# A modulation GEMV moves from GpSimd to VectorE, and four products start on the K tiles that are ready

## The reference, cut to what matters

```python
c_act = jax.nn.silu(c)
mod = c_act @ w_mod[l] + b_mod[l]          # w_mod: 2 x 2048 x 6144
shift, scale, gate = jnp.split(mod, 3, axis=-1)
h = x * (1.0 + scale[:, None]) + shift[:, None]
# and once more for the shared keys and values:
mod = c_act @ w_mod_kv + b_mod_kv          # 2048 x 4096
```

## Time and profile before

| what | value |
|---|---|
| median of three runs | 2972.42 us |
| span of the profiled execution (first to last instruction) | 2965.1 us |
| TensorE matmul busy | 2702.1 us, 91% |
| VectorE busy | 1774.0 us, 60% |
| ScalarE busy | 1222.6 us, 41% |
| GpSimd busy | 1637.6 us, 55% |
| moved by DMA | 604.67 MB, mean 204 GB/s |

### The profile page before, as it was taken

How to read it: one execution, slowest core, us unless ns; L and a number is a source line. 1 busy time by engine, 2 the same in 40 slices (tenths; PEclk the granted TensorE clock), 3 DMA queues, 4 the chain that set the end, 5 groups by cost and what they waited for, 6 DMA issues and landing times.

```text
span 2965.1 us, 37109 instructions
## 1 busy us (share of the span) xinstructions
PE 2702.1 (91%) x12005; PEld 2128.3 (72%) x12005; DVE 1774.0 (60%) x1786; ACT 1222.6 (41%) x1575; POOL 1637.6 (55%) x1060
## 2 busy tenths in 40 slices
PE   7987999998899888888888999998999879999987
PEld 6765787876677666666666777766788768888876
DVE  5789867757455555455545666655457556545645
ACT  4354333335333433333333333333458444444643
POOL 6986777774038999999989877798200000000000
PEclk9999999999999999999999999999999989999999
DMA  7776676776466777777676767766654536565453
GB/s 228 221 227 215 204 236 198 212 226 226 152 189 216 223 226 224 223 223 222 219 224 224 241 224 244 226 225 223 210 163 145 177 109 207 181 210 172 125 184 132
DMA packets 312714, 604.67 MB, mean 204 GB/s; under 512 B 26590, under 2 KB 28644, under 8 KB 310668
## 3 DMA queue, kind: packets, MB, share of 16 engines
q1 hardware_dynamic: 301628, 571.92, 61.5%
q10 hardware_dynamic: 10960, 31.10, 2.8%
HBM read 592.31 MB, written 10.62 MB: 203 GB/s over the span
## 4 chain that ended last, share of the span: by engine, by line
PE 42%; POOL 36%; issue 9%; DVE 8%; DMA 2%; ACT 2%; POOLq 1%; SPq 1%; DVEq 0%; ACTq 0%
POOL gemv_w L497 19%; POOL gemv_acc L507 14%; PE bank L566 12%; PE bank L568 11%; PE bank L567 11%; DVE w_lo L1649 3%; PE bank L654 2%; POOL gemv_acc L495 1%; PE bank L530 1%; POOL gemv_lo L511 1%; DVE sq L1795 1%; POOL gemv_hi L505 1%; DMA gemv_w<-in_kv_w_mod 1%; DMA raw<-in_w_ffn_down 1%; ACT w_hi L1067 1%
## 5 line engine op out<-in xcount | busy, mean ns | idle before, releaser
L1649 DVE TENSOR_TENSOR w_lo<-raw,w_hi 128x1024 fp32r<-128x1024 f32 x820 | 1252.2, 1532 | 1087.1 <-ACT w_hi L1067 1069.1
L1067 ACT CAST w_hi<-raw 128x1024 fp32r<-128x1024 f32 x820 | 860.1, 1050 | 1593.3 <-PE bank L568 815.1
L497 POOL TENSOR_TENSOR gemv_w<-gemv_w,small 128x512 f32<-128x512 f32 x480 | 735.9, 1533 | 183.8 <-DMA gemv_w<-in_w_mod 161.2
L507 POOL TENSOR_TENSOR gemv_acc<-gemv_acc,gemv_w 128x512 f32<-128x512 f32 x480 | 766.3, 1596 | 72.5 <-POOL gemv_w L497 68.9
L566 PE MATMUL bank<-w_hi,u_hi 128*128 128x512 f32 x1408 | 586.2, 416 | 93.2 <-DVE w_lo L1649 86.5
L568 PE MATMUL bank<-w_hi,u_lo 128*128 128x512 f32 x1408 | 564.2, 401 | 0.0
L567 PE MATMUL bank<-w_lo,u_hi 128*128 128x512 f32 x1408 | 563.7, 400 | 0.0
L566 PE MATMUL bank<-w_hi,s_hi 128*128 128x512 f32 x1280 | 520.8, 407 | 19.8 <-DVE w_lo L1649 16.6
L568 PE MATMUL bank<-w_hi,s_lo 128*128 128x512 f32 x1280 | 509.4, 398 | 0.0
L567 PE MATMUL bank<-w_lo,s_hi 128*128 128x512 f32 x1280 | 509.1, 398 | 0.0
L566 PEld LDWEIGHTS bank<-w_hi,u_hi 128*128 128x128 f32 x1408 | 269.4, 191 | 207.4 <-DVE w_lo L1649 138.7
(11 more groups left out here) (337 smaller groups left out, 2289.2 us busy)
## 6 DMA issues: line engine op xcount, KB each, us to landing
gemv_w<-in_w_mod SPq DMA_DIRECT2D x384, 256.0 KB, 3.0
raw<-in_w_in SPq DMA_DIRECT2D x176, 512.0 KB, 4.1
raw<-in_a_w_in SPq DMA_DIRECT2D x128, 512.0 KB, 3.9
raw<-in_w_ffn_gate SPq DMA_DIRECT2D x88, 512.0 KB, 4.3
raw<-in_w_ffn_up SPq DMA_DIRECT2D x88, 512.0 KB, 3.8
raw<-in_w_ffn_down SPq DMA_DIRECT2D x88, 512.0 KB, 4.2
gemv_w<-in_kv_w_mod SPq DMA_DIRECT2D x128, 256.0 KB, 3.0
raw<-in_kv_w SPq DMA_DIRECT2D x64, 512.0 KB, 3.7
```

The source lines that it names most:

```text
L497: pool.tensor_tensor(gemv_w[:, k % 2], gemv_w[:, k % 2], c_k, ALU.mult).then_inc(gemv_scaled, 1)
L507: ins = pool.tensor_tensor(gemv_acc[:], gemv_acc[:], gemv_w[:, k % 2], ALU.add)
L1067: act.copy(w_hi[:, s], raw[:, s]).then_inc(hi_done, 1)
L1649: dve.tensor_tensor(w_lo[:, s], raw[:, s], w_hi[:, s].bitcast(F32), ALU.subtract).then_inc(lo_done, 1)
```

## The change

The GEMV leaves GpSimd, which is then empty. VectorE does one step behind each split: one fused multiply and add from `gemv_w` into `gemv_acc` (a plain multiply for the first K tile; for the last one a second product for `gemv_hi`, and the subtraction for `gemv_lo`). SyncE's queue issues the GEMV load of step k behind the raw load two units later (`GEMV_LAG` = 2), and the last two of a chunk behind the first two raw loads of the next body or product. `load_gemv` itself, its wait included, is as before.

At the four borders `finish` is gone. The last chunk's drain stands at the end of the product like any other; its turn stands on TensorE behind unit 1, 2 or 3 of the next product, its cuts on ScalarE and VectorE before the splits of iteration 2 to 4, and TensorE waits for `turn_free` only before unit 6 (before unit 20 in down).

The core of the diff (the same is done on SyncE for every product, and for ffn, down and v2 on ScalarE and VectorE as it stands here for w_out):

```diff
@@ -325,7 +325,7 @@
...
-        gemv_scaled, gemv_cut = sem("gemv_scaled"), sem("gemv_cut")
+        gemv_cut = sem("gemv_cut")
...
+
+        GEMV_LAG = 2
...
@@ -432,87 +434,91 @@
                     sp.wait_ge(gemv_step, i * (pr.mods * KD) + (n * KD + k - 1))
                 sp.dma_start(gemv_w[:, k % 2], w[k * P:(k + 1) * P, ds(col + m * COLS, COLS)]).then_inc(gemv_landed[k % 2], 16)
...
-            def wide_body(pr, i, w, col, mod_w=None, mod_col=None):
+            def gemv_of(pr, i, mod_w, mod_col):
+
+                def issue(j):
+                    load_gemv(pr, i, j, mod_w, mod_col)
+
+                return issue
+
+            def tail_of(pr, gemv):
+
+                def issue(j):
+                    gemv(pr.units - GEMV_LAG + j)
+
+                return issue
+
+            def gemv_behind(j, gemv, tail):
+
+                if j >= GEMV_LAG:
+                    gemv(j - GEMV_LAG)
+                elif tail:
+                    tail(j)
+
+            def wide_body(pr, i, w, col, gemv, tail):
 
                 half = pr.units // 2
                 for j in range(pr.units):
                     load(pr, i, j, w, j % half, col + (j // half) * COLS)
-                    load_gemv(pr, i, j, mod_w, mod_col)
+                    gemv_behind(j, gemv, tail)
+
...
             pr = products["qkv"]
-            wide_body(pr, 0, w_in[0], 0, w_mod_2[0], 0)
+            gemv0 = gemv_of(pr, 0, w_mod_2[0], 0)
+            wide_body(pr, 0, w_in[0], 0, gemv0, None)
             with sp.Fori(1, pr.bodies) as i:
-                wide_body(pr, i, w_in[0], i * 2 * COLS, w_mod_2[0], i * COLS)
+                wide_body(pr, i, w_in[0], i * 2 * COLS, gemv_of(pr, i, w_mod_2[0], i * COLS),
+                          tail_of(pr, gemv_of(pr, i - 1, w_mod_2[0], (i - 1) * COLS)))
+            last = tail_of(pr, gemv_of(pr, pr.bodies - 1, w_mod_2[0], (pr.bodies - 1) * COLS))
             pr = products["spill"]
...
+            none = gemv_of(pr, 0, None, None)
+            two_weights(pr, 0, (w_branch_gdn, w_branch_moba), none, last)
+            with sp.Fori(1, pr.bodies) as i:
+                two_weights(pr, i, (w_branch_gdn, w_branch_moba), none, None)
...
-        @block.gpsimd
-        def _(pool):
-            pool.wait_ge(signal("c_ready"), 1)
-
-            def gemv_chunk(i):
-
-                for k in range(KD):
-                    pool.wait_ge(gemv_landed[k % 2], i * (8 * KD) + 16 * (k // 2 + 1))
-                    c_k = c_act[:, k:k + 1].broadcast_to([P, COLS])
-                    if k == 0:
-                        if not isinstance(i, int):
-                            pool.wait_ge(gemv_cut, i * 2)
-                        ins = pool.tensor_tensor(gemv_acc[:], gemv_w[:, 0], c_k, ALU.mult)
-                    else:
-                        pool.tensor_tensor(gemv_w[:, k % 2], gemv_w[:, k % 2], c_k, ALU.mult).then_inc(gemv_scaled, 1)
-                        pool.wait_ge(gemv_scaled, i * (KD - 1) + k)
-                        pool.wait_ge(gemv_step, i * KD + k)
-                        if k == KD - 1:
-
-                            if not isinstance(i, int):
-
-                                pool.wait_ge(mod_stored, i * 16)
-                            pool.tensor_tensor(gemv_hi[:], gemv_acc[:], gemv_w[:, k % 2], ALU.add).then_inc(gemv_cut, 1)
-                            pool.wait_ge(gemv_cut, i * 2 + 1)
-                        ins = pool.tensor_tensor(gemv_acc[:], gemv_acc[:], gemv_w[:, k % 2], ALU.add)
-                    ins.then_inc(gemv_step, 1)
-
-                pool.wait_ge(gemv_step, i * KD + KD)
-                pool.tensor_tensor(gemv_lo[:], gemv_acc[:], gemv_hi[:].bitcast(F32), ALU.subtract).then_inc(gemv_cut, 1)
-
-            gemv_chunk(0)
-            with pool.Fori(1, MOD_CHUNKS) as i:
-                gemv_chunk(i)
...
@@ -549,13 +555,15 @@
                     src.parity = (first + q) % 2
                     turn(i * pr.turns + (first + q), src)
 
-            def chunk(pr, i, x, hi, lo, units, between=None):
+            def chunk(pr, i, x, hi, lo, units, between=None, cut_by=None):
 
 
                 if not (isinstance(i, int) and pr.body0 + i == 0):
                     pe.wait_ge(drained[x], i * 2 + 2 * pr.body0)
                 for u in range(units):
                     j = x * units + u
+                    if cut_by and j == cut_by[0]:
+                        pe.wait_ge(turn_free, cut_by[1])
...
@@ -870,49 +874,58 @@
             branch_body(0)
             with pe.Fori(1, pr.bodies) as i:
                 branch_body(i)
-            turn_mixed(pr.bodies - 1)
-            pe.wait_ge(turn_free, pr.turn0 + pr.bodies * pr.turns)
+
+            def last_mixed(j, pr=pr):
+                if j == 1:
+                    turn_mixed(pr.bodies - 1)
+
+            mixed_cut = (6, pr.turn0 + pr.bodies * pr.turns)
...
+            def last_x(name, dest):
+
+                pr = products[name]
                 c = 2 * pr.bodies - 1
                 pe.wait_ge(drained[c % 2], 2 * (pr.body0 + c // 2 + 1))
                 turn_x(products[dest], c)
-                pe.wait_ge(turn_free, products[dest].turn0)
...
+                    if j == 2 and first:
+                        last_x("w_out", "ffn")
+                    elif j == 3 and not first:
                         turn_stage(pr, i - 1, 1)
 
-                chunk(pr, i, 0, u2_hi, u2_lo, pr.units // 2, due)
+                chunk(pr, i, 0, u2_hi, u2_lo, pr.units // 2, due, (6, pr.turn0) if first else None)
...
-            turn_stage(pr, pr.bodies - 1, 1)
-            pe.wait_ge(turn_free, pr.turn0 + pr.bodies * pr.turns)
...
-            turning_x("down", hid_hi, hid_lo, "v2", lambda: mod_columns(0))
+            def down_first(j, pr=pr):
+
+                if j == 3:
+                    turn_stage(pr, pr.bodies - 1, 1)
+                if j == products["down"].units // 2 - 1:
+                    mod_columns(0)
+
+            turning_x("down", hid_hi, hid_lo, "v2", down_first, (KF // 2 - 2, pr.turn0 + pr.bodies * pr.turns))
...
-            plain("v2", s_hi, s_lo)
+            plain_body("v2", 0, s_hi, s_lo, lambda j: j == 2 and last_x("down", "v2"), (6, products["v2"].turn0))
+            plain_body("v2", 1, s_hi, s_lo)
...
@@ -1648,6 +1677,36 @@
                 dve.wait_ge(hi_done, i * pr.units + (pr.unit0 + RING + j + 1))
                 dve.tensor_tensor(w_lo[:, s], raw[:, s], w_hi[:, s].bitcast(F32), ALU.subtract).then_inc(lo_done, 1)
 
+            def gemv(pr, i, j):
+
+                if not pr.mods:
+                    return
+                part = pr.units // pr.mods
+                m, k = j // part, j % part
+                if k >= KD:
+                    return
+                n = pr.mod0 + m
+                c_k, w_k = c_act[:, k:k + 1], gemv_w[:, k % 2]
+                dve.wait_ge(gemv_landed[k % 2], i * (pr.mods * 8 * KD) + (n * 8 * KD + 16 * (k // 2 + 1)))
+                if k == 0:
+                    if not (isinstance(i, int) and i * pr.mods + n == 0):
+                        dve.wait_ge(gemv_cut, i * (pr.mods * 2) + 2 * n)
+                    dve.tensor_scalar(gemv_acc[:], w_k, c_k, None, ALU.mult).then_inc(gemv_step, 1)
+                    return
+                dve.wait_ge(gemv_step, i * (pr.mods * KD) + (n * KD + k))
+                if k == KD - 1:
+                    if not (isinstance(i, int) and i * pr.mods + n == 0):
+
+                        dve.wait_ge(mod_stored, i * (pr.mods * 16) + 16 * n)
+                    dve.scalar_tensor_tensor(out=gemv_hi[:], in0=w_k, scalar=c_k, in1=gemv_acc[:], op0=ALU.mult,
+                                             op1=ALU.add).then_inc(gemv_cut, 1)
+                dve.scalar_tensor_tensor(out=gemv_acc[:], in0=w_k, scalar=c_k, in1=gemv_acc[:], op0=ALU.mult,
+                                         op1=ALU.add).then_inc(gemv_step, 1)
+                if k == KD - 1:
+                    dve.wait_ge(gemv_step, i * (pr.mods * KD) + (n * KD + KD))
+                    dve.wait_ge(gemv_cut, i * (pr.mods * 2) + (2 * n + 1))
+                    dve.tensor_tensor(gemv_lo[:], gemv_acc[:], gemv_hi[:].bitcast(F32), ALU.subtract).then_inc(gemv_cut, 1)
+
             def body(name, i, drain, between=None, limit=UNITS, finish=None):
 
 
@@ -1656,10 +1715,14 @@
                 for j in range(pr.units):
                     if between:
...
                     if between:
                         between(j)
-                    if finish and j == pr.units - 2:
+                    ending = finish and j == pr.units - 2
+                    if ending:
+                        gemv(pr, i, j)
                         finish()
                     if not isinstance(i, int) or pr.unit0 + i * pr.units + RING + j < limit:
                         split(pr, i, j)
+                    if not ending:
+                        gemv(pr, i, j)
                     if j % half == half - 1 and not (finish and j == pr.units - 1):
```

(58 more changed lines are left out.)

69 lines of the change are left out of this document (38 added, 31 removed).

## The result

The changed kernel takes 5024.61 us (median of four runs, 5021.69 to 5027.45) against 2972.04 us for the kernel before (median of four): ratio 1.690, 95% interval 1.688 to 1.692. The forecast was 5009 us, slower, in a range of 4750 to 5360.

The account below looks back on a forecast made before the run. SyncE's one in-order queue carries weights and GEMV loads, so TensorE, 91% busy, waits; after the change 500 rounds of 7.7 us (3850) + 22 + 1129 outside = 5001, plus 7.3 above the span: 5009 us, range 4750 to 5360.

Parts of the forecast that it names:

- The closed loop: SyncE's queue and VectorE's order: next raw load waits for the previous unit's landing, cast, split and GEMV step; chance 0.62.
- The round: One unit through that loop, from GEMV issue to step done: 7.7 us, bounds 7.3 to 8.4, where TensorE needs 2.93.
- The links: Raw loads each held by the split before, from qkv to q2: 500 at 7.7 us, 3850 us.
- free runs: Four stretches of 8 units in down without GEMV steps, outside the loop: 17 us each, 68 us.
- Rival (C): TensorE joins the loop in spill at the lower clock: 64 us more, 5073 us; chance 0.25.
- the rounding products: VectorE's one more product of 0.69 us ahead of the counted step in each of 32 chunks: 22 us.
- (A): Loop not closed, GEMV fits VectorE's idle time, weights flow at TensorE's pace: 2794 us, faster; chance 0.05.
- (B): Order wrong by one, two raw loads in flight per round: 3.85 us a unit, 3083 us; chance 0.04.
- (D): The extra wait is always met and the pace stays: 2972 us; chance 0.01.
- the queue's release: SyncE's queue no longer late, weights at TensorE's pace in qkv, w_out, ffn, down, v2 and k2: gain 148 us.
- The borders: Four idle stretches of 38 us between products; only 7.4 us credited, at the border from branch to w_out.
- What surrounds the span: Median of the runs taken as 7.3 us above the profile page's span: 5001 becomes 5009 us.

Follow-up runs that it names:

- lags four and six: Changed kernel with each GEMV load four or six units behind its raw load instead of two: 2777.61 us with four, 2775.87 us with six.
- lag three: Changed kernel with each GEMV load three units behind its raw load instead of two: 3185.69 us.
- the last experiment: Changed kernel with GEMV loads three units behind, but their wait for the step made ahead of the raw load of that position: 4670.46 us.

## Why the prediction was right, point by point

**The closed loop** was read off the program order and is there as described: one raw load per round, never two; undone by lags four and six, halved by lag three and (in the FFN) by another order on VectorE, kept by the last experiment.

**The round.** 7.7 us forecast, bounds 7.3 to 8.4. Measured between two raw loads in the first FFN body, 1795.28 - 1787.98 = 7.30; over the whole FFN 7.76 a unit. The fused step was priced 0.69 from another line, and 0.05 before it; it takes 0.745, of which 0.09 lies over the end of the split, so it adds 0.66 where 0.74 was forecast. In the first body, which is written out and not in a loop, the GEMV load goes 0.04 us after the step's end and the raw load 0.38 after it. Over the whole FFN these are 0.15 and 0.57 by the mean, against 0.15 and 0.60 forecast, and that is most of why this body is quicker than the rest. From the issue of a raw load to its cast are 4.07 us by the mean in the FFN and 4.25 in spill, where the forecast had 3.8 + 0.09: the term that was too small. By the median the landing took 3.8 to 4.2 (instruction, count, KB, median us to landing), beside the earlier trace rows:

```profile
gemv_w<-in_w_mod SPq DMA_DIRECT2D x384, 256.0 KB, 2.7
raw<-in_w_in SPq DMA_DIRECT2D x176, 512.0 KB, 4.2
...
raw<-in_w_ffn_gate SPq DMA_DIRECT2D x88, 512.0 KB, 4.0
raw<-in_w_ffn_up SPq DMA_DIRECT2D x88, 512.0 KB, 3.8
```

**The links.** The split of a unit is counted on L1678 (length of the stretch, busy time and count, which leaves out units 0 to 3):

```profile
0.00:1418.90 1418.90, 213.28 (x175) 0.76 0.36 113
0.00:1570.20 1570.20, 254.68 (x209) 0.78 0.37 116
0.00:3282.40 3282.40, 526.60 (x431) 0.76 0.35 109
0.00:3672.00 3672.00, 616.73 (x505) 0.76 0.35 112
0.00:4147.20 4147.20, 692.70 (x567) 0.76 0.35 111
```

| stretch, by splits | forecast | measured |
|---|---|---|
| unit 4 to 178, 174 links | 1347 | 1418.9 - 40.7 = 1378.2 |
| 178 to 212, branch | 149.8 | 1570.2 - 1418.9 = 151.3 |
| 212 to 434, 222 links | 1719 | 3282.4 - 1570.2 = 1712.2 |
| 434 to 508, 42 links and 4 free runs | 393 | 3672.0 - 3282.4 = 389.6 |
| 508 to 570, 62 links | 480 | 4147.2 - 3672.0 = 475.2 |
| from unit 570 | 870.8 | 5019.9 - 4147.2 = 872.7 |

(The forecast column is the text's 7.7 a link and 0.69 a chunk's end, with 11, 14, 3 and 4 chunk ends in the linked stretches.) All rows but the first are within 7 us. The first is 31 us over, and all of it is in spill: qkv's links, from the split of unit 4 to that of unit 48, took 340.4 us, and 340 follow from the forecast's terms. The other rows together are 12 us under, so the sum hits closer (0.3%) than its largest row does, and that part is luck.

**Rival (C)**, that TensorE joins the loop in spill at the lower clock, had 0.25 and 64 us. The clock fell as it said, to 0.76 in spill. But TensorE did not join. In the FFN five casts waited for it, 29.9 us in all, and of ScalarE's waits in spill (us in total, times, longest),

```profile
ACT w_hi L1088 <- DMA raw<-in_w_in: 801.7, 127, 9.8
```

nearly all the idle time before a cast ended with a landing, in 127 of 128 units, and none with a matmul. Spill was over the forecast by (7.98 - 7.7) x 128 = 36 us (5.5 of them are the rounding products, which the forecast counted apart). The landings of its raw loads (L421, 380 to 1402):

```profile
DMA to landing us min/median/max: 3.6/4.2/8.1
```

A landing of 4.2 us in place of 3.8 is enough for that. It could have been had beforehand: the same view of the kernel before (L419, 192 to 716) also gives a median of 4.2 in spill, and the forecast took its 3.8 from one load of qkv. The other traffic of that product (the spilled stages, the reloads of rows) is my reading of why; no run here took it away.

In the loop the lower clock had no price, since a unit at it still fits the round. In the FFN of the change the twelve matmuls of one unit, from 2406.16 to 2411.65, take 0.63 us each behind the first (granted clock 0.50), and those of the next, from 2413.71, 0.39 to 0.40 us behind the first (granted clock 1.00). The Trainium skill, "TensorE: Matmul & The Clock Gate", section on HAM oscillation, has such a loop start every tile at the low clock. The trace agrees for the mean (0.73 in the FFN) but not for every unit, as the second of these two shows.

No raw load's median in this trace is under 3.6 us. The Trainium skill, "DMA: Bandwidth & Descriptors", section on the anatomy of one DMA, would give an estimate of 3.2 us for 512 KB, and with it the sum would have been some 300 us too low; the measurement decides for the rows.

**Rivals (A), (B), (D)** did not come. (A)'s figure, 2794 us, is near what the same two ideas give when the loop is open: 2775.87 us with lag six. Its two steps from 2972 were the queue's release (148 forecast, 2973.4 - 2797.7 = 176 measured) and the borders (30 forecast, 19 to 22 measured).

**The borders** were priced at 7.4 us; without them the change takes 9 us longer, by one run.

**What surrounds the span.** I put 7.3 us on top of the span, the gap between the page and the median. The device time of the profiled run of the changed kernel is only 1.8 us above its span; the rest of 7.3 was the difference of one run from another. In a forecast this size those 5 us decide nothing.

## What to carry to other kernels

When work moves from one engine to another, every wait for that work moves with it. Ask of each queue that holds such a wait what it holds up, and write down what stands ahead of the awaited instruction in the new engine's program. Where that includes something that needs the very load held up, the ring of buffers is one deep, however many slots it has. A lag chosen as the least that does not lock was the slowest of the four tried: each of the next two units of lag put one more load in flight and together they took 5025 us to 2778, under the kernel before; two more changed nothing.

## What the runs showed that I had not expected

A raw load that has the queue nearly to itself landed only a little sooner, or no sooner. In the FFN the median over all raw loads fell from 4.1 us (985 to 1592, at 223 GB/s) to 3.8 (1780 to 3145, at 101 GB/s); in spill it stayed at 4.2, with the data rate down from 222 to 114 GB/s. The 4.3 that the prediction took for the FFN of before was one of its two weights; the other, `w_ffn_up`, had 3.8. In the changed kernel's products without GEMV loads (from 4193 on) the median is 3.7. To issue the raw load ahead of the GEMV load did not bring it there either: in the last experiment the FFN's median is 3.9, with a GEMV load 0.56 us behind each raw load, which accounts for a round of 7.05 us and not 6.9. What the 0.1 to 0.5 us above 3.7 are due to is not shown.

The fused multiply and add with both tensors in SBUF takes 745 ns for 512 columns, and 478 for 256: halving this operation saved 36% and not half.
